# Two attention stages reordered: copies ahead of exponents, waits by head, negated scores, one multiplication on GpSimd

## The chip, the cores and the metric

One core of a Trainium2 chip runs the whole program. Its engines run side by side, each through its own queue of instructions: TensorE (PE), VectorE (DVE), ScalarE (ACT), GpSimd (POOL) and SyncE (SP), which issues most of the DMAs. They wait for each other on semaphores. The metric is the device time of one execution in microseconds (us). Before the change it is 3049.75 us, the median of 3 runs (3048.73 to 3050.3).

## The reference

The input is `x` of 512 tokens by 1024. A first block of two layers runs over it, each with a mixer, a cross attention and an MLP. The mixer of layer 0 has two self attentions, and these are the first stage that the change touches:

```python
# a: 4 heads, each with two maps (c = 0, 1) of 64 columns, values of 128 columns
p = softmax(where(causal, q_c @ k_c.T * scale, -inf))
out_a = (p[:, :, 0] - lam * p[:, :, 1]) @ va          # then an rmsnorm of each row
# b: 8 heads of 64 columns, keys chosen by an index (top_k)
p = softmax(where(chosen & causal, q @ k.T * scale, -inf)); out_b = p @ vb
```

A second block follows: modulation from `c`, an mLSTM mixer beside an attention with 8 heads of 64 columns over all 512 keys with a bias by distance (the second stage that the change touches), an output product, and 16 experts that choose 64 tokens each:

```python
xin = h[idx]; hid = silu(xin @ w_gate) * (xin @ w_up)
y = (hid @ w_down) * gates; x = x + gate2 * zeros.at[idx].add(y)
```

All is float32. The weights of the experts are 16 x 3 matrices of 1024 x 2048, some 403 MB, which are read once.

## The kernel before

The program is a row of blocks. In a block each engine has its own list of instructions, and at its end all engines meet. Weights come through a ring of four slots of 2 MB (`Program.prefetch`), and the order of the work on each engine is written out by hand.

**Attention.** `attend_steps` does a list of steps. A step is one tile of 128 queries for two things at a time (e = 0, 1): in "apart" steps the two maps of one head, whose outputs are kept apart and joined later, else two heads. Step s does in turn:

- PE `scores(s)`: two products into PSUM banks 0 and 1, or 2 and 3, by the parity of s. It waits until `peak(s - 2)` has read these banks.
- DVE `peak(s)` (L661): `tensor_tensor_reduce` adds the bias (causal mask or distance), scales, writes the scores to SBUF (`probs`) and takes the row maximum, once for each e. A small instruction (L665) then multiplies the two maxima by -1, after a wait for the one in front (`vlink`).
- ACT `exponent(s)` (L745): exp(score - maximum) for each e, with the row sums.
- DVE `mix(s)`, only for steps that aren't apart (L672, L675): the reciprocal of the sums, then both heads' probabilities multiplied by it.
- PE `turn(s)` (L606): the probabilities transposed 128 x 128 at a time into banks 4 (e = 0) and 5 (e = 1). It waits for the probabilities of s, and for both copies of step s - 1, which read the same two banks.
- ACT and DVE `copy_turned(s)` (L754, L682): bank 4 to SBUF by ACT; bank 5 by ACT in even steps and by DVE in odd ones.
- PE `values(v)` (L620 apart, L626 else): the product with the values, once for each apart step and once for two steps else. DVE `finish(v)` (L689, L693 to L697) moves the result out.

The steps are staggered by `lag`: in its round s, PE does scores(s), turn(s - lag) and then values of a group that ended at s - lag - 1. DVE does peak(s), mix(s - 1), its copy of s - lag, finish. ACT does exponent(s), then its copies of s - lag, and in the first stage a row of squares (`square`).

There are two calls. `e_att` (in `even_mixer`, lag 3) has 32 steps: 16 apart (4 heads by 4 tiles of queries) and 16 not apart (4 pairs of heads by 4 tiles); tile i of queries has (i + 1) x 128 keys, so widths go 128, 256, 384, 512 and start again. While the second 16 run, DVE also does the rmsnorm of the first half's rows (`row_scale`, `scale_rows`). `s_att` (in `second_block`, lag 2) has 16 steps, none apart, all of width 512.

**Experts.** `experts` follows `s_att`. It streams 8 pairs of experts x 24 chunks of 2 MB through 8 slots. The output product of the mixer and the router run first, in the same block. Of the last pair, `scatter_half(0)` (L2945) adds the first half of the columns of the result back to the token rows: PE spreads it (four tiles of tokens), DVE adds (L3029, `add_half`). It stands between the two last groups of products of the last column half. DVE's order is: first half gated, its four adds, second half gated (L3060), its four adds.

## Time and profile before

| What | Value |
|---|---|
| Median of 3 runs | 3049.75 us |
| Profiled execution, own time | 3044.21 us |
| Its span, first to last instruction | 3042.4 us |
| PE busy | 2820.1 us (93%) |
| DVE, ACT, POOL busy | 779.3, 431.1, 56.6 us |
| DMA | 570.71 MB, 188 GB/s over the span |
| Mean granted TensorE clock | 0.981 of full speed |
| `e_att`, first scores to the next stage's first product | 264.80 to 369.01 us |
| `s_att`, the same | 1954.24 to 2025.07 us |

The page has a line of tenths for each engine in 40 slices of the span. DMA stands at 9 from slice 29 on (427 to 429 GB/s), the stage of the experts, and at 0 to 3 in most others. The busy share of PE hides stretches in which it runs on with short gaps, as in the two attention stages; these are seen in the views by stretch and by time.

### The profile page before, as it was taken

How to read it: one execution, taken by the hardware profiler on the slowest of the kernel's cores; microseconds unless marked ns; L12 is line 12 of the kernel's file. 1: busy time of each engine (PE TensorE's matmuls, PEld its weight loads, DVE VectorE, ACT ScalarE, POOL GpSimd, SP SyncE). 2: the span in 40 equal slices, each digit the busy share in tenths (PEclk: the TensorE clock that was granted, in tenths of full speed). 3: DMA queues.
4: the chain of work that ended last, by engine and by line, in shares of the span. 5: the costliest groups of instructions: out<-in, count | busy, mean ns of one | idle time of the engine just before them, and what ended most of it. 6: DMA issues, size and time to landing. Idle time of an engine off the chain costs nothing. (4 is left out here: it accounts for less than half of the span.)

```text
span 3042.4 us, 24643 instructions
## 1 busy us (share of the span) xinstructions
PE 2820.1 (93%) x9741; PEld 1277.8 (42%) x9741; DVE 779.3 (26%) x1998; ACT 431.1 (14%) x950; POOL 56.6 (2%) x149
## 2 busy tenths in 40 slices
PE   8998898999999998999999899787999889889888
PEld 4545544444444444444544444444333323233232
DVE  2398623011001314340000244644111111111111
ACT  2124412000001002211000122231000000000000
POOL 0000000000000000110000010000000000000000
PEclk9999999999999999999999999898999999999999
DMA  7230012122212201682121111222999999999998
GB/s 279 69 111 14 1 42 83 61 77 83 83 62 80 83 28 56 210 287 83 56 83 56 55 57 56 76 84 103 427 428 428 428 428 429 428 428 428 428 428 374
DMA packets 107472, 570.71 MB, mean 188 GB/s; under 512 B 11578, under 2 KB 12364, under 8 KB 82940
## 3 DMA queue, kind: packets, MB, share of 16 engines
q1 hardware_dynamic: 99248, 538.64, 44.0%
q0 software_dynamic: 6768, 29.43, 2.8%
q10 hardware_dynamic: 1372, 1.51, 0.2%
q8 instruction: 54, 0.88, 0.1%
q14 instruction: 30, 0.25, 0.0%
HBM read 567.43 MB, written 6.32 MB: 189 GB/s over the span
## 5 line engine op out<-in xcount | busy, mean ns | idle before, releaser
L205 PE MATMUL banks<-hT,ring 128*128 128x512 f32 x1024 | 441.5, 594 | 5.1 <-PEq L298 5.1
L205 PEld LDWEIGHTS banks<-hT,ring 128*128 128x128 f32 x1024 | 195.0, 191 | 250.4 <-issue 250.4
L2902 PE MATMUL banks<-ring,second_arena 128*64 128x512 f32 x1024 | 232.0, 597 | 29.7 <-DMA ring<-in_w_up 16.0
L324 PE MATMUL banks<-ring,m_u 128*128 128x512 f32 x512 | 220.3, 592 | 1.6 <-PEq L178 1.6
L1984 PE MATMUL banks<-ring,second_arena 128*128 128x512 f32 x512 | 220.6, 593 | 0.0
L2902 PE MATMUL banks<-second_arena 128*64 128x512 f32 x768 | 174.5, 598 | 17.5 <-DMA second_arena<-in_w_gate 15.0
L324 PEld LDWEIGHTS banks<-ring,m_u 128*128 128x128 f32 x512 | 97.0, 190 | 123.4 <-issue 123.4
L1984 PEld LDWEIGHTS banks<-ring,second_arena 128*128 128x128 f32 x512 | 97.5, 191 | 121.7 <-issue 121.7
L2902 PEld LDWEIGHTS banks<-ring,second_arena 128*64 128x64 f32 x1024 | 70.0, 136 | 184.0 <-issue 133.6
L2902 PE MATMUL banks<-ring,mod 128*64 128x512 f32 x512 | 114.7, 596 | 12.7 <-DMA ring<-in_w_down 12.7
L3022 DVE TENSOR_TENSOR x_rows<-banks,x_rows 128x512 f32<-128x512 f32 x64 | 44.3, 692 | 282.4 <-PE banks L2938 282.4
L1749 PE MATMUL banks<-hT,ring 128*128 128x512 f32 x256 | 110.4, 592 | 2.5 <-PEq L298 2.5
L1523 PE MATMUL banks<-ring,hT 128*128 128x512 f32 x256 | 111.1, 594 | 0.9 <-PEq L887 0.9
L2902 PEld LDWEIGHTS banks<-second_arena 128*64 128x64 f32 x768 | 51.2, 136 | 133.3 <-issue 89.5
L2902 PE MATMUL banks<-second_arena,mod 128*64 128x512 f32 x384 | 84.6, 595 | 2.9 <-DMA second_arena<-in_w_down 2.9
L3051 DVE TENSOR_TENSOR mod<-banks,mod 128x512 f32<-128x512 f32 x32 | 22.1, 691 | 244.5 <-PE banks L2902 244.5
L360 ACT ACTIVATE x_square<-x_rows 128x1024 f32<-128x1024 f32 x20 | 21.1, 1057 | 401.5 <-DVE x_rows L348 217.1
L1899 DVE SCALAR_TENSOR_TENSOR mod<-second_arena,mod 128x1536 f32<-128x1536 f32 x32 | 58.2, 1819 | 75.0 <-DMA second_arena<-in_w_ada 75.0
L1749 PEld LDWEIGHTS banks<-hT,ring 128*128 128x128 f32 x256 | 48.5, 190 | 63.0 <-issue 63.0
L1523 PEld LDWEIGHTS banks<-ring,hT 128*128 128x128 f32 x256 | 48.6, 191 | 62.0 <-issue 61.2
L2902 PE MATMUL banks<-hT,second_arena 128*64 128x512 f32 x256 | 58.3, 597 | 14.9 <-DMA hT<-in_w_up 14.9
L2938 PE MATMUL banks<-second_arena 128*128 128x512 f32 x128 | 72.0, 645 | 0.0
(563 smaller groups left out, 2897.0 us busy)
## 6 DMA issues: line engine op xcount, KB each, us to landing
ring<-in_w_up SPq DMA_DIRECT2D x48, 2048.0 KB, 30.5
ring<-in_w_down SPq DMA_DIRECT2D x48, 2048.0 KB, 33.7
ring<-in_w_gate SPq DMA_DIRECT2D x32, 2048.0 KB, 34.0
second_arena<-in_w_gate SPq DMA_DIRECT2D x32, 2048.0 KB, 30.7
second_arena<-in_w_down SPq DMA_DIRECT2D x24, 2048.0 KB, 35.4
second_arena<-in_w_up SPq DMA_DIRECT2D x16, 2048.0 KB, 32.4
hT<-in_w_up SPq DMA_DIRECT2D x16, 2048.0 KB, 33.8
second_arena<-in_w_ada POOLq DMA_DIRECT2D x32, 768.0 KB, 4.7
```

The lines of the kernel that those rows point to most:

```text
L205: mm = nc.tensor.matmul(o, w[:, k, a:z], src[:, ka, 0:ntok], start=(ka == 0), stop=(ka == kc * kgroups - 1))
L324: mm = nc.tensor.matmul(g.psum[:, b * NT + m, :], act[:, ka, m * P:m * P + P], w[:, k, :], start=(ka == 0), stop=(ka == kc * kgroups - 1))
L360: g.alink(nc.scalar.activation(square[:], g.x[:, t, :], ACT.Square, accum_out=g.row_stats[:, 0, t:t + 1]))
L1523: mm = nc.tensor.matmul(bank, a[:, k, m * P:m * P + P], w[:, k, :], start=(k == 0), stop=(k == kc - 1))
L1749: mm = nc.tensor.matmul(o, w[:, k, m * P:m * P + P], g.hT[:, k, :], start=(k == 0), stop=(k == KD - 1))
L1899: nc.vector.scalar_tensor_tensor(o, w[:, n % 2, :], cs[:, k:k + 1], o, ALU.mult, ALU.add).then_inc(added.up(), 1)
L1984: mm = nc.tensor.matmul(g.psum[:, b * NT + m, :], u[:, ka, m * P:m * P + P], w[:, k, :], start=(ka == 0), stop=(ka == KD * kgroups - 1))
L2902: mm = nc.tensor.matmul(g.psum[64 * e:64 * e + 64, bank, :], lhs(q * half + k)[:, 64 * e:64 * e + 64], w[:, e, k, :], start=first, stop=last)
L2938: nc.tensor.matmul(g.psum[:, 6 + u % 2, :], sg[:, tt * P:tt * P + P], y[:, c * BANK:c * BANK + BANK], start=True, stop=True).then_inc(s_ba ...
L3022: nc.vector.tensor_tensor(xs, g.psum[:, 6 + u % 2, :], xs, ALU.add).then_inc(s_add.up(), 1)
L3051: nc.vector.tensor_tensor(hid[:, b % 2, :], g.psum[:, (b % 2) * 2 + 1, :], act_g[:, b % 2, :], ALU.mult).then_inc(s_hid.up(), 1)
```

## The change

In `attend_steps`: ACT does its copies of step s - lag before the exponents of step s. DVE's copies are left only in apart odd steps; in all others ACT makes both. PE waits for the copy of bank 4 before it turns e = 0, and for that of bank 5 only before e = 1. `peak` scales by -scale and takes a minimum, so that its result is the negated maximum; L665 and its wait go, and the exponent is taken with scale = -1. In steps that aren't apart DVE multiplies only head 0 by the reciprocal; a new list of GpSimd does head 1, and PE waits for both. The argument `warm`, which no caller sets, goes. In `experts`, two of the four tiles of `scatter_half(0)` move behind the last group of products.

```diff
--- before.py
+++ after.py
@@ -534,7 +534,7 @@
                     at += a
 
 
-def attend_steps(g, name, steps, probs, keyed, scale, lag, warm=0, rows=None):
+def attend_steps(g, name, steps, probs, keyed, scale, lag, rows=None):
 
     nc = g.nc
     S, B = len(steps), 4
@@ -548,18 +548,17 @@
     mixed_before = [sum(not st["apart"] for st in steps[:s + 1]) for s in range(S)]
     s_scores, s_peak, s_probs, s_mixed, s_turned, s_out, s_read, s_copied_a, s_copied_v = (g.counter(n) for n in (
         "scores", "peak", "probs", "mixed", "turned", "out", "out_read", "moved_a", "moved_v"))
+    s_inverse, s_mixed_pool = g.counter("inverse"), g.counter("rooted")
     s_joined, s_squared, s_scaled, s_rows_turned = (g.counter(n) for n in ("joined", "squared", "scaled", "x_turned"))
 
-    def copied_by_act(s):
-        return s + 1 + s // 2 + 1
-
-    def copied_by_dve(s):
-        return (s + 1) // 2
-
-    def wait_copied(eng, s):
-        eng.wait_ge(*s_copied_a.at(copied_by_act(s)))
-        if s:
-            eng.wait_ge(*s_copied_v.at(copied_by_dve(s)))
+    by_dve = [st["apart"] and s % 2 for s, st in enumerate(steps)]
+
+    def wait_copied(eng, s, e):
+        n = sum(by_dve[:s + 1])
+        if e and by_dve[s]:
+            eng.wait_ge(*s_copied_v.at(n))
+        else:
+            eng.wait_ge(*s_copied_a.at(2 * s + e + 1 - sum(by_dve[:s])))
 
     def into(s, e):
         step = steps[s]
@@ -599,9 +598,10 @@
                         pe.wait_ge(*s_probs.at(s + 1))
                     else:
                         pe.wait_ge(*s_mixed.at(mixed_before[s]))
-                    if s:
-                        wait_copied(pe, s - 1)
+                        pe.wait_ge(*s_mixed_pool.at(mixed_before[s]))
                     for e in range(2):
+                        if s:
+                            wait_copied(pe, s - 1, e)
                         for j in range(step["nk"] // P):
                             mm = nc.tensor.transpose(g.psum[:, 4 + e, j * P:j * P + P], probs[:, s % B, e, j * P:j * P + P],
                                                      g.ident[:])
@@ -609,7 +609,8 @@
 
                 def values(v):
                     step = steps[ops[v][-1]]
-                    wait_copied(pe, ops[v][-1])
+                    for e in range(2):
+                        wait_copied(pe, ops[v][-1], e)
                     if v >= 2:
                         pe.wait_ge(*s_read.at(v - 1))
                     n = step["nk"] // P
@@ -630,9 +631,6 @@
                 for s in range(S + lag + 1):
                     if s < S:
                         scores(s)
-                    if s == 0:
-                        for _ in range(warm):
-                            nc.tensor.matmul(g.psum[:, 7, :], g.ident[:], g.causal[:, 0:BANK], start=True, stop=True)
                     if 0 <= s - lag < S:
                         turn(s - lag)
                     if s - lag - 1 in last_of:
@@ -646,6 +644,14 @@
                                                          g.ident[:])
                             mm.then_inc(s_rows_turned.up(), 1)
 
+            @block.gpsimd
+            def _(pool):
+                for s in range(S):
+                    if not steps[s]["apart"]:
+                        pool.wait_ge(*s_inverse.at(mixed_before[s]))
+                        p = probs[:, s % B, 1, 0:steps[s]["nk"]]
+                        nc.gpsimd.tensor_scalar(p, p, st[:, s % 8, 3, 1:2], None, ALU.mult).then_inc(s_mixed_pool.up(), 1)
+
             @block.vector
             def _(dve):
                 v_ = nc.vector
@@ -659,21 +665,19 @@
                         if "ready" in step:
                             dve.wait_ge(*step["ready"][e])
                         ins = v_.tensor_tensor_reduce(probs[:, s % B, e, 0:step["nk"]],
-                                                      g.psum[:, (s % 2) * 2 + e, 0:step["nk"]], step["bias"][e], scale,
-                                                      NEG * 10, ALU.add, ALU.max, st[:, s % 8, 0, e:e + 1])
-                    g.vlink(ins)
-                    v_.tensor_scalar(st[:, s % 8, 1, :], st[:, s % 8, 0, :], -1.0, None, ALU.mult).then_inc(s_peak.up(), 1)
+                                                      g.psum[:, (s % 2) * 2 + e, 0:step["nk"]], step["bias"][e], -scale,
+                                                      -NEG * 10, ALU.add, ALU.min, st[:, s % 8, 1, e:e + 1])
+                    ins.then_inc(s_peak.up(), 1)
 
                 def mix(s):
                     step = steps[s]
                     if step["apart"]:
                         return
                     dve.wait_ge(*s_probs.at(s + 1))
-                    g.vlink(v_.reciprocal(st[:, s % 8, 3, :], st[:, s % 8, 2, :]))
-                    for e in range(2):
-                        p = probs[:, s % B, e, 0:step["nk"]]
-                        ins = v_.tensor_scalar(p, p, st[:, s % 8, 3, e:e + 1], None, ALU.mult)
-                    ins.then_inc(s_mixed.up(), 1)
+                    v_.reciprocal(st[:, s % 8, 3, :], st[:, s % 8, 2, :]).then_inc(s_inverse.up(), 1)
+                    dve.wait_ge(*s_inverse.at(mixed_before[s]))
+                    p = probs[:, s % B, 0, 0:step["nk"]]
+                    v_.tensor_scalar(p, p, st[:, s % 8, 3, 0:1], None, ALU.mult).then_inc(s_mixed.up(), 1)
 
                 def copy_turned(s):
                     dve.wait_ge(*s_turned.at(2 * s + 2))
@@ -722,7 +726,7 @@
                         peak(s)
                     if 1 <= s <= S:
                         mix(s - 1)
-                    if 0 <= s - lag < S and (s - lag) % 2:
+                    if 0 <= s - lag < S and by_dve[s - lag]:
                         copy_turned(s - lag)
                     if s - lag - 2 in last_of:
                         finish(last_of[s - lag - 2])
@@ -742,7 +746,7 @@
                     act.wait_ge(*s_peak.at(s + 1))
                     for e in range(2):
                         p = probs[:, s % B, e, 0:step["nk"]]
-                        ins = nc.scalar.activation(p, p, ACT.Exp, bias=st[:, s % 8, 1, e:e + 1],
+                        ins = nc.scalar.activation(p, p, ACT.Exp, bias=st[:, s % 8, 1, e:e + 1], scale=-1.0,
                                                    accum_out=st[:, s % 8, 2, e:e + 1])
                     ins.then_inc(s_probs.up(), 1)
 
@@ -764,12 +768,12 @@
                 if rows:
                     act.wait_ge(*s_joined.at(1))
                 for s in range(S + lag):
+                    if s >= lag:
+                        copy_turned(s - lag, 0)
+                        if not by_dve[s - lag]:
+                            copy_turned(s - lag, 1)
                     if s < S:
                         exponent(s)
-                    if s >= lag:
-                        copy_turned(s - lag, 0)
-                        if not (s - lag) % 2:
-                            copy_turned(s - lag, 1)
                     if rows and 0 <= s - lag - 3 < apart:
                         square(s - lag - 3)
                 if rows:
@@ -2938,10 +2942,10 @@
                 nc.tensor.matmul(g.psum[:, 6 + u % 2, :], sg[:, tt * P:tt * P + P], y[:, c * BANK:c * BANK + BANK],
                                  start=True, stop=True).then_inc(s_back.up(), 1)
 
-            def scatter_half(c):
+            def scatter_half(c, tiles=range(NT)):
 
                 pe.wait_ge(s_y.sem, (pairs - 1) * 2 + (s_y.base + c + 1))
-                for tt in range(NT):
+                for tt in tiles:
                     nc.tensor.matmul(g.psum[:, last_banks[c][tt], :], sg[:, tt * P:tt * P + P],
                                      y[:, c * BANK:c * BANK + BANK], start=True, stop=True).then_inc(s_back.up(), 1)
 
@@ -2964,8 +2968,8 @@
                     for kg in range(2):
                         pair_of_groups(i, 4 * nf + 4 * b + 2 * kg, 6 + b, lambda k: hT[:, kg * KD + k, :],
                                        kg == 0, kg == 1, last and b == kg == 1)
-                        if last and b == 1 and kg == 0:
-                            scatter_half(0)
+                        if last and b == 1:
+                            scatter_half(0, (2 * kg, 2 * kg + 1))
                     if b == 0 and not last:
                         gather(i + 1)
 
```

## Rows read from the trace of the kernel before

**Rows 1.** Chain that ended last, in order of time: start us, us, what.

```profile
2272.85 32.10 DMA ring<-in_w_down
```

**Rows 2.** Stretches: us, then each engine busy (x instructions), PEclk, DMA share, GB/s.

```profile
2110.00:2125.00 15.00, 13.68 (x84) 11.01 (x86) 4.44 (x12) 0.00 (x0) 0.00 (x0) 0.79 0.00 1
2125.00:2272.00 147.00, 145.22 (x672) 52.52 (x670) 19.14 (x32) 9.62 (x14) 0.00 (x0) 1.00 1.00 424
```

**Rows 3.** Stretches of attention, same view; engines PE, PEld, DVE, ACT, POOL.

```profile
305.76:317.75 11.99, 10.29 (x78) 7.97 (x77) 9.72 (x44) 7.42 (x31) 0.00 (x0) 1.00 0.01 2
317.75:333.59 15.84, 13.01 (x83) 8.11 (x82) 12.89 (x58) 8.06 (x31) 0.00 (x0) 0.89 0.00 1
333.59:346.06 12.47, 8.21 (x47) 4.67 (x45) 11.23 (x42) 6.62 (x22) 0.00 (x0) 0.86 0.01 2
346.06:356.73 10.67, 8.35 (x62) 4.86 (x61) 9.42 (x39) 6.50 (x22) 0.00 (x0) 1.00 0.00 0
...
1978.87:1986.57 7.70, 6.09 (x43) 3.38 (x41) 5.69 (x18) 4.49 (x12) 0.00 (x0) 1.00 0.00 0
```

**Rows 4.** Instructions in order of time, first stage: start us, us, engine, line.

```profile
308.97 0.49 PE L592 MATMUL banks<-e_KTb,e_QTb 64*128 64x128 f32 x4
...
309.91 0.42 ACT L754 ACTIVATE e_keyed<-banks 128x128 f32<-128x128 f32 x2
...
310.42 0.63 PE L606 MATMUL banks<-ident,e_probs 128*128 128x128 f32 x4 [0.96 <-ACT e_probs L745]
```

**Rows 5.** Instructions in order of time, one pair of steps of the second stage.

```profile
1978.87 1.13 PE L592 MATMUL banks<-second_arena 64*128 64x512 f32 x4
...
1980.05 0.69 DVE L661 CUSTOM_DVE_ANT_0 second_arena<-banks,second_arena 128x512 f32<-128x512 f32 x1 [1.86 <-PE banks L592]
...
1981.27 0.08 DVE L661 DVE_READ_ACCUMULATOR2_ANT s_att_stats<- 128x1 f32 x1
1981.39 0.17 DVE L665 TENSOR_SCALAR s_att_stats<-s_att_stats 128x2 f32<-128x2 f32 x1
1981.47 0.16 DVE L672 RECIPROCAL s_att_stats<-s_att_stats 128x2 f32<-128x2 f32 x1
1981.60 0.72 ACT L745 ACTIVATE second_arena<-second_arena,s_att_stats 128x512 f32<-128x512 f32 x1 [1.88 <-DVE s_att_stats L665]
1981.66 0.88 DVE L675 TENSOR_SCALAR second_arena<-second_arena,s_att_stats 128x512 f32<-128x512 f32 x2
...
1983.02 0.58 ACT L754 ACTIVATE mod<-banks 128x512 f32<-128x512 f32 x1
...
1983.69 1.06 PE L606 MATMUL banks<-ident,second_arena 128*128 128x128 f32 x8 [1.61 <-ACT mod L754]
...
1984.69 1.95 PE L626 MATMUL banks<-mod,second_arena 128*64 128x256 f32 x16
...
1986.57 1.13 PE L592 MATMUL banks<-second_arena 64*128 64x512 f32 x4
```

**Rows 6.** GpSimd: in order of time beside DVE; one group by line; a DVE tile view.

```profile
1914.27 2.29 DVE L2309 TENSOR_TENSOR second_arena<-second_arena,s_head_stats 128x2048 f32<-128x2048 f32 x1
1914.42 2.29 POOL L2165 TENSOR_SCALAR_AFFINE_SELECT second_arena<-second_arena 128x128 f32<-128x128 f32 x1 [9.33 <-DVE second_arena L2349]
...
L909 POOL TENSOR_SCALAR_AFFINE_SELECT causal<-causal 128x512 f32<-128x512 f32 x1 | 0.6, 612 | 0.1
...
L675 DVE TENSOR_SCALAR e_probs<-e_probs,e_att_stats x32: 279/383/486, 313.5 to 359.7; 128x128 f32<-128x128 f32 x8, 128x256 f32<-128x256 f32 x8, 128x384 f32<-128x384 f32 x8, 128x512 f32<-128x512 f32 x8
```

**Rows 7.** Instructions in order of time, the end of the kernel.

```profile
3024.04 3.70 PE L2945 MATMUL banks<-second_arena 128*128 128x512 f32 x8
...
3027.67 3.65 PE L2902 MATMUL banks<-second_arena,mod 128*64 128x512 f32 x16
...
3034.81 0.69 DVE L3060 TENSOR_TENSOR second_arena<-banks,mod 128x512 f32<-128x512 f32 x1 [6.34 <-PE banks L2902]
...
3035.56 3.70 PE L2945 MATMUL banks<-second_arena 128*128 128x512 f32 x8 [0.80 <-DVE second_arena L3060]
```

## The prediction

> **What bounds the kernel now.** I read the chain of waits first. From 2272.85 us on it is the stream of expert weights that sets the pace: PE is released by a landing each time [rows 1]. So the question is whether time won earlier reaches the end. The view by stretches answers it: DMA stands still from 2110 to 2125 us (share 0.00), and from 2125 on it runs full (1.00) without a break [rows 2]. The stream therefore starts when PE, in the expert stage, frees its first slot, and not before. Whatever ends earlier ahead of it moves the stream as one piece. The same holds between the two attention stages, which are PE's own product stages with weights loaded ahead. A microsecond won in attention is a microsecond at the end.
>
> Then the attention stages, by stretches cut at the same point of each round of four steps. In the first half of `e_att` a round is 11.99 us with PE busy 10.29; in the second half three rounds are 15.84, 12.47 and 10.67 us, with PE busy 13.01, 8.21 and 8.35; in `s_att` a pair of steps is 7.70 us with PE busy 6.09 [rows 3]. No engine is full; the time is in waits that go round. Last, the instructions in order of time show which. In `e_att` scores of width 128 start at 308.97 and the next turn only at 310.42, after a wait of 0.96. Its missing input is a copy of the step before, which ACT starts at 309.91, behind two long exponents, though PE had finished that turn by 308.97 [rows 4]. In `s_att` it is the same: ACT copies at 1983.02, behind the exponents that began at 1981.60, and PE turns at 1983.69 after 1.61 us idle [rows 5].
>
> **The change, part by part.** Each term is a saving (minus) or a cost (plus) in us.
>
> *First stage, apart steps (4 rounds).* No GpSimd work here. With ACT's copies ahead of the exponents, a copy starts when its turn is done. The wait by head lets PE turn e = 0 while bank 5 is still being copied, and the path from scores to exponent loses L665. What is late next: PE itself, which has 10.29 busy us in a round, against DVE 9.72 and ACT 7.42 [rows 3]. DVE loses four L665 of 0.17 [rows 5]. So a round goes to about 10.29: 4 x (11.99 - 10.29) = -6.8. If the exponents pushed back by the copies were late for PE three steps on, some of it would stay; lag 3 leaves room.
>
> *First stage, steps not apart (4 rounds, three whole ones in the rows).* DVE now loses, per round, four L665 (0.17), four multiplications (0.28 to 0.49, median 0.38 [rows 6]) and two copies: some 2.2 us besides the copies. DVE's 12.89, 11.23 and 9.42 busy us [rows 3] become at most 10.7, 9.0 and 7.2. ACT takes the two copies, and the pair at 309.91 and the single one at 1983.02 put a copy between 0.2 and 0.6 us [rows 4, 5]; ACT's 6.62 becomes 7.8 at most, still under PE. The bound of each round is then the larger of PE and DVE: 13.01, 9.0, 8.35. That saves 2.8 + 3.5 + 2.3 = 8.6. The rmsnorm of the rows is a serial run on DVE that PE waits for, and it stays, so I take -7.0 of it. The fourth round, filling and draining: the last copies and the last mix are shorter for PE, -1.
>
> *Second stage (16 steps).* The loop after the change, per pair, by [rows 5]: scores to the first DVE operation 1.18 (1978.87 to 1980.05); two reductions to the start of the reciprocal, now without L665, 1.30 (1980.05 to 1981.27, and 0.08); reciprocal to multiplication 0.19; the slower of the two multiplications 1.0 (next paragraph) and 0.05 to PE; turn 1.00 (1983.69 to 1984.69); values 1.88 (to 1986.57), after which come the next scores of this kind. Together 6.60. PE's own work is 6.09, ACT's 4.49 plus one copy of 0.58, DVE's 5.69 less two L665, two multiplications and a copy. So the loop sets it: 7.70 - 6.60 = 1.10 a pair, over seven and a half pairs: -8.2.
>
> *The GpSimd multiplication.* The trace has no such operation. The nearest row is a one-input select of 128x512 with 0.612 [rows 6]. One row shows what happens beside DVE: a select of 128x128 took 2.29 us while DVE ran an operation of 2.29 on two SBUF tensors, and ended 0.15 after it [rows 6]. DVE's multiplication goes from 0.28 at 128 columns to 0.49 at 512, 0.5 ns a column, two columns a cycle of the one-column rate of 0.69 us at 512 that the reduction has [rows 5, 6]. If that form also shuts GpSimd out, head 1 starts when head 0 is done: 0.44 + 0.56 = 1.0 after the reciprocal, no better than the 0.88 that DVE takes for both [rows 5]. If not, it is 0.61 to 0.65. Ends: 0.6 (the loop falls to 6.2, -11.2 in the second stage) and 2.3 (the blocked row; the loop is 7.9, +1.5). I take 1.0. In the first stage lag 3 gives the multiplication a whole further step, so it costs nothing there below about 2.5 us.
>
> The Trainium skill bears on this (SBUF — State Buffer, Who interferes with whom): a DVE instruction in a 2-port mode and a GpSimd instruction exclude each other for their whole length, and `tensor_scalar` can be in such a mode. The blocked row agrees for two SBUF inputs. By the rule the GpSimd part wins nothing here, and without it the second stage would stand at -11.2 rather than -8.2.
>
> *The end.* Before, the four products of `scatter_half(0)` run from 3024.04 to 3027.67 and PE idles while L3060 runs at 3034.81 [rows 7]. Two of them (0.9 each) go behind the last products. PE then ends these 1.8 earlier and spreads tiles 2 and 3 until about 3034.8. But DVE adds all four tiles before it gates the second half: L3060 waits for the add of tile 3, which starts at about 3034.8 and takes 0.6 to 0.7. The last spread starts at 3036.2 instead of 3035.56: +0.65. If the last landing holds PE up, it loses up to the 1.8 as well: +2.5. I take +0.7.
>
> *Sum.* -6.8 - 7.0 - 1.0 - 8.2 + 0.7 = -22.3. The profiled execution took 3044.2 (span 3042.4), so it would be 3021.9. It lies 5.5 below the median of 3049.75, and I carry the difference over: 3027.5.
>
> The granted clock is at the lower level for part of these stages (0.89 and 0.86 in two rounds [rows 3]) after PE idled. Shorter idles may bring it back, and a new one may cost it; two or three us either way, not in the sum.
>
> **The rivals.**
>
> *A, GpSimd free of DVE and the clock steadier.* The loop is then 6.2 a pair and near PE's 6.09: 3 more, and 2 to 4 from the clock. For it: the reductions, which read one tensor from PSUM, should not stand in GpSimd's way. Against: the blocked row. Time 3021.
>
> *B, half of it.* The waits between engines that my loops leave out, ACT's later exponents and the new double wait before each turn (PE's whole queue stands behind it: turn, values, and the scores two steps on) take half of the gain, so -12: 3038. For it: DVE and ACT would be above 80% busy in some rounds, which leaves little slack. Against: the loops add up to the rounds before.
>
> *C, slower.* One mechanism: GpSimd's multiplication. In `s_att` each us of it beyond 1.0 costs 7.5 in all; in `e_att` it starts to count at about 2.5 and then costs some 8 per us. At 2.0 the second stage has lost its gain; at about 3.2 it costs 16 there and 6 in the first, and the whole change stands at zero. At 3.6 it is 3055. For it: only the blocked select of 2.29. Against: 0.612 for the same width.
>
> *D, nothing reaches the end.* The expert stream decides and the start of the stream doesn't move, or the change doesn't shorten the rounds. 3050.5. Against: DMA share 0.00 before 2125 [rows 2].
>
> **How the numbers follow.** Forecast (-17 to -27): 0.58, A 0.16, B 0.16, C 0.05, D 0.05. A measurement of this kernel can tell about 0.2%, 6.1 us, from no change. Faster by more: the forecast, A, and B but for its weak end, 0.90; within: D and the rest of B, 0.06; slower: 0.04. The range runs from A's better end, 3018, to B's weaker one, 3041; some 0.06 lie below and 0.12 above.
>
> **What would show it.** In the profile after: rounds of `e_att` of 10.2 to 10.6 us in the first half and 8.5 to 10.5 in the second; pairs of `s_att` of 6.6 (6.2 would show rival A); ACT's copies (now ahead of L745) starting within 0.1 us of their turn; GpSimd's multiplication ending about 1.0 after the reciprocal, behind DVE's; no gap of 1.4 us after the scores of width 128. L3060 starts behind an add of L3029. The stages between should keep their length, and the expert stage too, within 1 us. A GpSimd row above 2 us, a DMA that no longer stands still before the stream, or rounds still at 12 and 7.7 would prove the prediction wrong.

## The result, and the profile after

The changed kernel took 3024.74 us (median of 4 runs, 3020.18 to 3028.71) against 3050.03 us of the kernel before on the same chip (3048.73 to 3051.51): a ratio of 0.9916 [0.9899, 0.9934], 25.3 us less. It ran twice more later, at 3026.08 us (ratio 0.9929 [0.9912, 0.9946]) and 3023.19 us (0.9917 [0.9903, 0.993]). The forecast was 3027.5, 22.3 us less.

The profiled execution took 3026.5 us, with a span of 3024.8. I cut both spans at the same four instructions: first scores of `e_att`, first product of the stage behind it, first scores of `s_att`, first product behind it.

| Stretch, us | before | after | change | forecast |
|---|---|---|---|---|
| ahead of `e_att` | 264.80 | 265.21 | +0.41 | 0 |
| `e_att` | 104.21 | 82.33 | -21.88 | -14.8 |
| between the two, untouched | 1585.23 | 1592.69 | +7.46 | 0 |
| `s_att` | 70.83 | 67.28 | -3.55 | -8.2 |
| from there to the end | 1017.33 | 1017.29 | -0.04 | +0.7 |
| span | 3042.4 | 3024.8 | -17.6 | -22.3 |

So the sum came out near the forecast, but its terms did not: the first stage gave half as much again, the second less than half. The two errors (7.1 too small, 4.7 too large) have opposite signs and partly cancel in the sum, which is luck. And the stretch that nothing in the change touches is 7.5 us longer in this pair of profiles.

The view by stretches of the kernel after, for the second and fourth round of apart steps, the three rounds behind them, a pair of steps of `s_att`, each whole stage and the stretch between (us, then busy time of PE, PEld, DVE, ACT, POOL, then the granted clock, DMA share and GB/s):

```profile
276.77:286.98 10.21, 10.21 (x77) 7.97 (x76) 8.37 (x35) 7.82 (x32) 0.00 (x0) 1.00 0.01 2
297.19:307.40 10.21, 10.21 (x77) 7.97 (x76) 8.74 (x38) 7.82 (x32) 1.71 (x2) 1.00 0.01 2
307.40:315.73 8.33, 8.33 (x61) 5.64 (x60) 7.66 (x32) 6.04 (x27) 4.08 (x4) 1.00 0.00 1
315.73:326.47 10.74, 8.54 (x62) 4.95 (x61) 10.15 (x42) 7.94 (x28) 5.99 (x4) 1.00 0.01 2
326.47:334.96 8.49, 8.25 (x62) 4.87 (x61) 7.08 (x28) 7.16 (x25) 4.98 (x4) 1.00 0.00 1
1972.80:1980.29 7.49, 6.09 (x43) 3.38 (x41) 3.98 (x13) 4.97 (x13) 3.71 (x2) 1.00 0.00 0
265.21:347.54 82.33, 75.59 (x561) 53.36 (x561) 65.00 (x262) 61.41 (x218) 21.18 (x16) 1.00 0.01 1
347.54:1940.23 1592.69, 1530.30 (x4000) 722.65 (x4001) 339.76 (x789) 211.54 (x441) 50.07 (x107) 0.98 0.24 84
1940.23:2007.51 67.28, 53.03 (x321) 29.66 (x321) 32.44 (x104) 40.14 (x96) 29.84 (x17) 0.93 0.00 1
```

Against [rows 3]: a round of apart steps is 10.21 us and PE is busy in all of it (11.99 and 10.29 before). The pair of `s_att` went only from 7.70 to 7.49, and POOL is now busy 3.71 of it, two multiplications.

The three rounds behind it, 8.33, 10.74 and 8.49 us, can't be set against the 15.84, 12.47 and 10.67 of [rows 3]. Those three aren't cut at the same point of their rounds: they hold 83, 47 and 62 products of PE, those of the kernel after 61, 62 and 62. The same view of the kernel before, first its four last rounds, each from one set of scores of width 512 to the next (the last to the end of the stage) as in the view above, then its first round, the two halves of `e_att`, and `s_att`:

```profile
317.75:329.32 11.57, 9.88 (x61) 6.54 (x60) 9.07 (x39) 6.28 (x26) 0.00 (x0) 0.85 0.00 1
329.32:343.46 14.14, 9.87 (x62) 5.73 (x61) 12.52 (x52) 6.62 (x22) 0.00 (x0) 0.88 0.01 2
343.46:354.72 11.26, 8.35 (x61) 4.86 (x60) 9.94 (x42) 6.72 (x23) 0.00 (x0) 1.00 0.00 0
354.72:369.01 14.29, 9.79 (x81) 7.01 (x81) 8.14 (x22) 6.42 (x17) 0.00 (x0) 1.00 0.00 1
264.80:281.76 16.96, 13.72 (x72) 8.88 (x72) 10.26 (x48) 9.56 (x34) 0.00 (x0) 0.76 0.01 1
264.80:317.75 52.95, 44.61 (x301) 32.81 (x301) 38.13 (x167) 32.62 (x124) 0.00 (x0) 0.92 0.01 1
317.75:369.01 51.26, 37.89 (x261) 24.14 (x261) 39.67 (x152) 26.03 (x87) 0.00 (x0) 0.93 0.00 1
1954.24:2025.07 70.83, 55.51 (x320) 30.52 (x321) 45.91 (x144) 36.14 (x88) 0.09 (x1) 0.89 0.00 1
```

So these rounds went from 11.57, 14.14, 11.26 and 14.29 to 8.33, 10.74, 8.49 and 12.58 (334.96 to 347.54). Of the first three, only the middle one still has PE waiting for more than 0.3 us. It holds DVE's rmsnorm, and DVE is busy for 10.15 of its 10.74. In order of time, PE waits in it first for DVE and then for GpSimd:

```profile
320.82 0.70 PE L591 MATMUL banks<-e_KTb,e_QTb 64*128 64x256 f32 x4 [0.69 <-DVE e_att_stats L667]
323.02 0.85 PE L606 MATMUL banks<-ident,e_probs 128*128 128x128 f32 x6 [1.50 <-POOL e_probs L653]
```

Compare the granted clock: 0.92 and 0.93 over the two halves of `e_att` before, 1.00 over the whole of it after. PE's busy time for the same instructions fell with it, from 82.50 (44.61 + 37.89) to 75.59. A part of that is no effect of the change. The first scores of the stage, the same 16 products, kept PE busy for 4.95 us before and 2.75 after, though the stage had hardly waited by then. In before's profile the clock stood at 0.50 (1.2 GHz) in the stage's first 3 us, in after's at 1.00 (2.4 GHz). These are the rows of before, then of after:

```profile
264.80 4.95 PE L592 MATMUL banks<-hT 64*128 64x128 f32 x16 [0.94 <-PEq L1503]
...
265.21 0.93 PE L591 MATMUL banks<-hT 64*128 64x128 f32 x8 [1.29 <-PEq L1507]
266.40 1.82 PE L591 MATMUL banks<-hT 64*128 64x384 f32 x8 [0.26 <-DVE e_att_stats L667]
```

The first turn follows 4.87 us after the stage's start before and 2.94 after, so some 1.9 of the 21.88 us belong to that one execution. Experiment 1 below, which has the change's order of copies, begins at 0.50 as well.

Instructions in order of time, `s_att` after (start us, us, engine, line; in brackets the idle time ahead and its releaser). These answer to [rows 5]:

```profile
1972.80 1.13 PE L591 MATMUL banks<-second_arena 64*128 64x512 f32 x4
...
1975.21 0.16 DVE L677 RECIPROCAL s_att_stats<-s_att_stats 128x2 f32<-128x2 f32 x1
1975.40 0.48 DVE L680 TENSOR_SCALAR second_arena<-second_arena,s_att_stats 128x512 f32<-128x512 f32 x1
1975.46 1.85 POOL L653 TENSOR_SCALAR second_arena<-second_arena,s_att_stats 128x512 f32<-128x512 f32 x1 [3.48 <-DVE s_att_stats L677]
...
1977.41 1.06 PE L606 MATMUL banks<-ident,second_arena 128*128 128x128 f32 x8 [1.40 <-issue]
...
1978.08 1.08 ACT L758 ACTIVATE mod<-banks 128x512 f32<-128x512 f32 x2 [1.04 <-PE banks L606]
1978.41 1.95 PE L627 MATMUL banks<-mod,second_arena 128*64 128x256 f32 x16
```

DVE's half is ready at 1975.88, GpSimd's at 1977.31, and PE turns at 1977.41 after 1.40 us idle. The row names "issue", but what ends just in front of it is GpSimd's half; a later profile of the same kernel (experiment 4) names it at the same place of an earlier pair:

```profile
1953.66 1.06 PE L606 MATMUL banks<-ident,second_arena 128*128 128x128 f32 x8 [1.40 <-POOL second_arena L653]
```

In the rows of the kernel after, ACT's copies are no longer late: they start at 1978.08, while the turn (1977.41 to 1978.47) still runs.

The end of the kernel after, against [rows 7]:

```profile
3005.56 1.98 PE L2949 MATMUL banks<-second_arena 128*128 128x512 f32 x4
3007.48 3.65 PE L2906 MATMUL banks<-second_arena,mod 128*64 128x512 f32 x16
...
3016.52 0.69 DVE L3033 TENSOR_TENSOR x_rows<-banks,x_rows 128x512 f32<-128x512 f32 x1 [0.17 <-PE banks L2949]
3017.12 0.68 DVE L3064 TENSOR_TENSOR second_arena<-banks,mod 128x512 f32<-128x512 f32 x1
...
3017.86 3.70 PE L2949 MATMUL banks<-second_arena 128*128 128x512 f32 x8 [1.38 <-DVE second_arena L3064]
...
3021.60 0.69 DVE L3033 TENSOR_TENSOR x_rows<-banks,x_rows 128x512 f32<-128x512 f32 x1 [0.17 <-PE banks L2949]
```

The gate L3064 starts right behind an add, as foreseen. From the first spread to the end of the last add it is 3022.29 - 3005.56 = 16.73 us; before, it was 15.94 (from 3024.04 to the last add's end at 3039.98).

### The profile page after: what moved, and what is told of

The parts are those of the page before. It is cut to its first block and busy times, and to the rows that moved or that the text cites. A ratio compares the mean times of both kernels' runs of the same rounds, so it can differ in the third digit from the quotient of the medians.

```text
span 3024.8 us, 24597 instructions
## 1 busy us (share of the span) xinstructions
PE 2816.1 (93%) x9741; PEld 1275.1 (42%) x9741; DVE 753.2 (25%) x1902; ACT 437.9 (14%) x966; POOL 107.3 (4%) x181
## 5 line engine op out<-in xcount | busy, mean ns | idle before, releaser
L2906 PE MATMUL banks<-second_arena 128*64 128x512 f32 x768 | 174.5, 598 | 17.6 <-DMA second_arena<-in_w_gate 15.1
L2906 PE MATMUL banks<-hT,second_arena 128*64 128x512 f32 x256 | 58.3, 597 | 14.8 <-DMA hT<-in_w_up 14.8
```

Source lines behind the costliest of these rows:

```text
L2906: mm = nc.tensor.matmul(g.psum[64 * e:64 * e + 64, bank, :], lhs(q * half + k)[:, 64 * e:64 * e + 64], w[:, e, k, :], start=first, stop=last)
```

## The experiments

The theory after the first result: ACT's copies behind the exponents held PE up in both stages, and putting them first is most of the gain; in `s_att` GpSimd's multiplication of 1.86 us has taken the place of that wait. The rivals: the gain comes from the parts that shorten DVE's work (negation, multiplication), or the length of the multiplication does not matter. Except where it is said, each kernel is the changed one with one edit.

**1. Both multiplications on DVE.**

```diff
-                    p = probs[:, s % B, 0, 0:step["nk"]]
-                    v_.tensor_scalar(p, p, st[:, s % 8, 3, 0:1], None, ALU.mult).then_inc(s_mixed.up(), 1)
+                    for e in range(2):
+                        p = probs[:, s % B, e, 0:step["nk"]]
+                        ins = v_.tensor_scalar(p, p, st[:, s % 8, 3, e:e + 1], None, ALU.mult)
+                    ins.then_inc(s_mixed.up(), 1)
```

GpSimd's list and PE's wait for it go.

> The changed kernel, but VectorE multiplies both heads again and GpSimd does nothing in attention. Stage lengths are from the first scores to the next block's first product: first stage 104.2 us before and 82.3 after, second stage 70.8 and 67.3. Theory 1 (GpSimd's 1.86 us a multiplication sets the loop of the second stage): its pair of steps falls from 7.49 us to 5.58 + 0.88 = 6.46, at least PE's 6.09; the second stage falls by some 7 to 59 to 61 us, the first stage grows by 0 to 3 because VectorE is fuller beside the row work. Total 3 to 8 us faster than the changed kernel. Theory 2 (taking work off VectorE is where the gain comes from): the second stage grows to 69 or more and the first by over 5; total 5 or more slower than the changed kernel.

Measured: 3020.15 us (4 runs, 3018.66 to 3020.42), ratio 0.9904 [0.9887, 0.992]; `e_att` 85.45, `s_att` 57.03 us. In order of time, one pair of `s_att`:

```profile
1968.84 1.13 PE L591 MATMUL banks<-second_arena 64*128 64x512 f32 x4
...
1971.44 0.88 DVE L672 TENSOR_SCALAR second_arena<-second_arena,s_att_stats 128x512 f32<-128x512 f32 x2
...
1972.37 1.09 PE L605 MATMUL banks<-ident,second_arena 128*128 128x128 f32 x8 [0.33 <-DVE second_arena L672]
...
1975.27 1.13 PE L591 MATMUL banks<-second_arena 64*128 64x512 f32 x4
```

The pair is 6.43 us (1975.27 - 1968.84), PE's idle ahead of the turn 0.33 instead of 1.40. The two multiplications together are done 0.88 after they start, GpSimd's one after 1.85. So GpSimd's multiplication costs `s_att` 10 us (67.28 - 57.03; 8.4 and 11.0 against the two later profiles of the changed kernel), while the stage without it would have gained 13.8. Theory 1 is borne out, and by more than it named: the second stage fell below its 59 to 61 us. The 85.45 of `e_att` holds the low clock at its start, as before's does; experiment 12, the same kernel, took 83.58.

**2. Exponents first, as before the change.**

```diff
+                    if s < S:
+                        exponent(s)
                     if s >= lag:
                         copy_turned(s - lag, 0)
                         if not by_dve[s - lag]:
                             copy_turned(s - lag, 1)
-                    if s < S:
-                        exponent(s)
```

> The changed kernel, but ScalarE does the exponents of step s ahead of its copies of the step before by lag, as before the change. Theory 1 (the order on ScalarE is the main gain of the first stage): the first stage goes back from 82.3 to 90 to 96 us and the waits of 1.0 and 0.7 us of PE in each round of four steps return; the second stage stays within 1.5 us of 67.3, as GpSimd holds it anyway. Total 8 to 12 slower than the changed kernel. Theory 2 (the gain is from the negation that went, the wait by head and the multiplication that moved): first stage below 86.

Measured: 3043.22 us (8 runs, 3037.89 to 3044.5), ratio 0.998 [0.997, 0.9991]; `e_att` 94.30, `s_att` 69.28. The old wait is back in both stages:

```profile
306.34 0.19 ACT L749 ACTIVATION_READ_ACCUMULATOR e_probs<-e_probs,e_att_stats 128x1 f32 x1
306.43 0.42 ACT L758 ACTIVATE e_keyed<-banks 128x128 f32<-128x128 f32 x2
...
306.83 0.63 PE L606 MATMUL banks<-ident,e_probs 128*128 128x128 f32 x4 [0.64 <-ACT e_keyed L758]
...
1977.50 1.06 PE L606 MATMUL banks<-ident,second_arena 128*128 128x128 f32 x8 [1.45 <-ACT mod L758]
```

ACT copies at 306.43, behind the exponent of 512 columns, and PE turns once the copy is done. The order of ACT's list alone is worth 17 us of the 25 (3043.22 against 3026.08 of the changed kernel on the same chip), more than the 8 to 12 expected. In `s_att` it is worth little while GpSimd is in the loop: the turn waits 1.45 for the copy or 1.40 for GpSimd.

**3. Both multiplications on GpSimd.**

```diff
-                        pe.wait_ge(*s_mixed.at(mixed_before[s]))
-                        pe.wait_ge(*s_mixed_pool.at(mixed_before[s]))
+                        pe.wait_ge(*s_mixed_pool.at(2 * mixed_before[s]))
```

GpSimd's list goes over e = 0 and 1, and DVE's multiplication goes.

> The changed kernel, but GpSimd multiplies both heads and VectorE none. It prices the multiplication without a VectorE one beside it. If VectorE's multiplication holds GpSimd off for its length, the first of each two GpSimd rows of 512 columns takes about 1.86 - 0.43 = 1.4 us where no other VectorE work lies beside it. If 1.86 is GpSimd's own time, both rows stay at 1.8 to 1.86. The second stage then pays two of them in its loop: pair 5.58 + 3.7 = 9.3 us, second stage 81 to 84 us; with 1.4 each 8.4 and 75 to 77 us.

Measured (one run): 3051.51 us; `e_att` 86.38, `s_att` 87.61. Groups of GpSimd's multiplication by form (busy us, mean ns | idle before), both on GpSimd:

```profile
L653 POOL TENSOR_SCALAR second_arena<-second_arena,s_att_stats 128x512 f32<-128x512 f32 x32 | 49.5, 1564 | 56.9 <-DVE s_att_stats L678 56.9
L653 POOL TENSOR_SCALAR e_probs<-e_probs,e_att_stats 128x384 f32<-128x384 f32 x8 | 10.2, 1290 | 5.9 <-DVE e_att_stats L678 5.9
L653 POOL TENSOR_SCALAR e_probs<-e_probs,e_att_stats 128x128 f32<-128x128 f32 x8 | 4.8, 606 | 280.3 <-DVE e_att_stats L678 280.3
```

And the same groups of the kernel after, where DVE multiplies beside it:

```profile
L653 POOL TENSOR_SCALAR second_arena<-second_arena,s_att_stats 128x512 f32<-128x512 f32 x16 | 29.7, 1854 | 56.7 <-DVE s_att_stats L677 56.7
...
L653 POOL TENSOR_SCALAR e_probs<-e_probs,e_att_stats 128x384 f32<-128x384 f32 x4 | 6.4, 1600 | 9.0 <-DVE e_att_stats L677 9.0
L653 POOL TENSOR_SCALAR e_probs<-e_probs,e_att_stats 128x128 f32<-128x128 f32 x4 | 3.2, 798 | 280.7 <-DVE e_att_stats L677 280.7
```

Without DVE's multiplication beside it GpSimd takes 1.56 us for 512 columns, with it 1.85. So 1.56 is its own time, and 0.29 is what DVE's multiplication of 0.48 adds. Neither expected case is what `s_att` shows: 87.61 lies above both (75 to 77 and 81 to 84). It is 20 us longer than with one multiplication on GpSimd. PE's busy time for the same products grew by 10 of them (53.03 to 63.22), with the granted clock at 0.81 over the stage (0.93 with one), which the expectation left out. The first stage, with its lag of three steps, grows by 3 to 4.

**4. The changed kernel once more.** No edit.

> The changed kernel once more, unaltered, on the chip of the three others, so that they can be compared with it. Stage lengths 82.3 and 67.3 us within 2, total within 4 of 3024.7; differences between executions should lie in stretches at the lower clock level elsewhere.

Measured: 3026.08 us (4 runs, 3025.81 to 3030.22), ratio 0.9929 [0.9912, 0.9946]; `e_att` 83.39, between 1592.60, `s_att` 65.47. A third time (run 11 below): 83.47, 1587.00 and 68.02. The stretch between, of the same kernel in its second and its third profile:

```profile
348.14:1940.74 1592.60, 1530.17 (x4001) 724.22 (x4001) 339.73 (x789) 211.55 (x441) 50.52 (x107) 0.98 0.24 84
```

```profile
349.32:1936.32 1587.00, 1524.64 (x4000) 720.26 (x4001) 339.46 (x789) 211.44 (x441) 50.48 (x107) 0.98 0.24 84
```

The same instructions differ by 5.6 us, and PE's busy time by 5.5. Over all profiles this stretch took 1585 to 1587 (before, 9, 10, 11) or 1592 to 1595 (the rest), and the unaltered changed kernel stands in both groups. So the +7.46 of the first table needs no effect of the change; whether a kernel makes one of the two lengths more likely, these profiles do not show.

**5. The kernel before, with nothing but the copies put first.** The edit is that of experiment 2, the other way round, in the kernel before.

> The kernel before, with one edit: ScalarE's copies of a step ahead of the exponents. Theory 1: this alone brings the first stage from 104.2 to 91 to 97 us, and the second from 70.8 to 66 to 69. Theory 2 (the parts only work together, or the order matters little): first stage above 100.

Measured (one run): 3032.74 us beside 3049.69 for before; `e_att` 93.61, `s_att` 63.29. In order of time, this kernel:

```profile
314.66 1.12 PE L606 MATMUL banks<-ident,e_probs 128*128 128x128 f32 x6 [1.58 <-DVE e_keyed L682]
...
1984.63 1.06 PE L606 MATMUL banks<-ident,second_arena 128*128 128x128 f32 x8 [1.21 <-DVE mod L682]
```

One reordering gives 17 us. What remains is DVE: in the steps that aren't apart PE waits for DVE's copy (L682), behind its two multiplications. The other parts together give some 6 more (3032.74 against 3026.42 of experiment 7, on the same chip). That is a sum of two signs: they take 10 to 11 us off `e_att`, and they make `s_att` 2 to 5 us longer (63.29 here, 65.47 to 68.02 with the whole change), since GpSimd's multiplication is one of them. In `e_att` the two are nearly additive: 104.21 - 93.61 = 10.6 and 104.21 - 94.30 = 9.9, together 20.5, and 20.7 to 21.9 were measured with both. Each of these differences holds the 1.9 us of before's low clock at the start.

**6. The negation kept as an instruction.**

```diff
-                                                      g.psum[:, (s % 2) * 2 + e, 0:step["nk"]], step["bias"][e], -scale,
-                                                      -NEG * 10, ALU.add, ALU.min, st[:, s % 8, 1, e:e + 1])
-                    ins.then_inc(s_peak.up(), 1)
+                                                      g.psum[:, (s % 2) * 2 + e, 0:step["nk"]], step["bias"][e], scale,
+                                                      NEG * 10, ALU.add, ALU.max, st[:, s % 8, 0, e:e + 1])
+                    g.vlink(ins)
+                    v_.tensor_scalar(st[:, s % 8, 1, :], st[:, s % 8, 0, :], -1.0, None, ALU.mult).then_inc(s_peak.up(), 1)
```

> The changed kernel with the maximum and the small multiplication by -1 back, with its wait. Theory 1: the second stage's loop gets 0.1 to 0.2 us a pair longer, 67.3 to 68.3; the first stage 1 to 2 us longer. Rival: in the first stage PE is the bound and nothing changes (below 0.5), the negation being off the path there.

Measured (one run): 3035.22 us, `e_att` 84.54, `s_att` 70.45, the stretch between 1594.61. The pair of `s_att`:

```profile
1978.30:1985.98 7.68, 6.08 (x43) 3.37 (x41) 4.30 (x15) 4.98 (x13) 3.71 (x2) 1.00 0.00 0
```

It is 0.19 longer than 7.49, so the instruction and its wait cost 1.4 us over seven and a half pairs. `e_att` is 2.2 longer than the 82.33 of the changed kernel; the granted clock is 1.00 over the stage in both, so the clock isn't what parts them. The 70.45 of `s_att` is above the 67.3 to 68.3 expected. The rest of that difference lies in stretches at the lower clock (0.90 over the stage, 0.93 in the changed kernel). Of the 8.8 us that this run lies above experiment 7 on the same chip, 3.2 are in `s_att` and 2.8 in the stretch between, which the edit doesn't touch; one run cannot price the instruction closer.

**7. PE waits for both copies before it turns.**

```diff
-                    for e in range(2):
-                        if s:
+                    if s:
+                        for e in range(2):
                             wait_copied(pe, s - 1, e)
+                    for e in range(2):
```

> The changed kernel, but PE waits for both copies of the step before ahead of its first transposition, as before the change. Theory 1: with the copies early this wait is nearly always over: both stages within 0.7 us of 82.3 and 67.3. Rival (the wait by head carries a part of the gain): the first stage is 2 to 4 us longer.

Measured (one run): 3026.42 us; `e_att` 83.61, `s_att` 67.28. `e_att` is 0.6 beyond the bound of theory 1 (83.0), but the changed kernel itself took 83.39 and 83.47 in its other profiles. So one run shows no difference: with the copies first, the wait by head brings nothing by itself here.

**8. DVE's copies kept in all odd steps.**

```diff
-    by_dve = [st["apart"] and s % 2 for s, st in enumerate(steps)]
+    by_dve = [s % 2 for s, st in enumerate(steps)]
```

> The changed kernel, but in steps that aren't apart VectorE makes the bank 5 copy of odd steps again. Theory 1: the second stage stays within 1 us of 67.3, since GpSimd holds its loop; the second half of the first stage is 1 to 3 us longer, as VectorE has the row work there. Rival: ScalarE's extra copy costs as much as it saves, and both stages stay within 0.5.

Measured (one run): 3030.63 us; `e_att` 84.33, `s_att` 67.31. In `s_att` nothing changes, since GpSimd still sets its loop; `e_att` is 2.0 longer than the 82.33 of the changed kernel, both at a granted clock of 1.00, as theory 1 had it (one run). Of the 4.2 us that its time lies above experiment 7 on the same chip, 2.7 are in the stretch between (1594.44 against 1591.78).

**9 to 12. GpSimd where it is covered, and the end mended.** Experiment 9 gives the second stage back to DVE (`rows` is set in the first stage only):

```diff
-                        pe.wait_ge(*s_mixed_pool.at(mixed_before[s]))
+                        if rows:
+                            pe.wait_ge(*s_mixed_pool.at(mixed_before[s]))
...
-                    if not steps[s]["apart"]:
+                    if rows and not steps[s]["apart"]:
...
+                    for e in range(1 if rows else 2):
```

Experiment 10 is 9 and, in `experts`, the gate ahead of two adds:

```diff
                     if last:
-                        add_half(b)
+                        if b:
+                            add_half(0, (2, 3))
+                        add_half(b, (0, 1) if b == 0 else range(NT))
```

Run 11 is the changed kernel, 12 is experiment 1 again, all on one chip.

> The changed kernel with GpSimd's multiplication kept in the first stage only; in the second stage DVE multiplies both halves, as before the change. Theory (a multiplication on GpSimd pays where three steps of lag cover its 1.86 us and costs where the loop contains it): the first stage keeps its 82.3 to 83.4 us, the second falls from 65.5 to 67.3 to 57.0, its pair from 7.48 to 6.44 us, so the profiled span is 3015.5 (3014 to 3018) and the ratio to the kernel before about 0.989. Rival (the first stage gains nothing from GpSimd either, since PE is full in its first half): the first stage stands at 84 to 85.5, and the time equals that of both halves on DVE everywhere, 3020.

> As the run with GpSimd in the first stage only, and in the last pair DVE gates the second half of the products before it adds tiles 2 and 3 of the first. Theory (the last spread waits for the gate, and the gate stood behind two adds that wait for late spreads): the gate L3064 starts as soon as PE ends its last products, the idle of 1.38 us ahead of the last spread shrinks to about 0.7, and from the first spread to the end of the last add it is about 16.0 us instead of 16.7; time 0.7 below the run without it. Rival (the late adds only move behind and end the kernel later): 16.7 or more, no gain.

> The changed kernel as it is, as the partner of the other three on this chip. Expected: ratio to the kernel before 0.9916 to 0.993, first stage 82 to 84 us, second stage 65 to 68.

> Both halves multiplied by DVE in both stages, once more, to tell it from the run with GpSimd in the first stage only. Theory (GpSimd takes 0.28 to 0.49 us a step off DVE in the second half of the first stage, where DVE is the busiest engine beside PE): the first stage is 1.5 to 3 us longer than with GpSimd, the second the same 57.0, so 3020 against 3017. Rival: no difference that five rounds can tell.

| Kernel | us | ratio to before (3049.2) | `e_att` | between | `s_att` |
|---|---|---|---|---|---|
| 9 GpSimd in `e_att` only | 3012.33 | 0.9882 [0.9867, 0.9897] | 84.94 | 1585.22 | 57.03 |
| 10 the same, gate first | 3009.72 | 0.9871 [0.9855, 0.9886] | 83.39 | 1586.86 | 57.03 |
| 11 changed kernel | 3023.19 | 0.9917 [0.9903, 0.993] | 83.47 | 1587.00 | 68.02 |
| 12 both on DVE | 3018.94 | 0.9895 [0.988, 0.991] | 83.58 | 1594.95 | 57.01 |

The end of experiment 10, in order of time:

```profile
3000.38 5.42 PE L2952 MATMUL banks<-second_arena 128*128 128x512 f32 x12
...
3000.50 0.69 DVE L3067 TENSOR_TENSOR second_arena<-banks,mod 128x512 f32<-128x512 f32 x1 [6.34 <-PE banks L2909]
3001.54 0.69 DVE L3036 TENSOR_TENSOR x_rows<-banks,x_rows 128x512 f32<-128x512 f32 x1 [0.35 <-PE banks L2952]
...
3005.84 0.69 DVE L3036 TENSOR_TENSOR x_rows<-banks,x_rows 128x512 f32<-128x512 f32 x1 [0.17 <-PE banks L2952]
```

The gate now runs while PE spreads tiles 2 and 3, and PE does all its last spreads without a gap. From first spread (2991.45) to the last add's end it is 15.08 us, against 16.73 of the change and 15.94 of before: 1.65 gained, where 0.7 was expected.

The second stage came out as expected (57.03). The theory that GpSimd's half gains 1.5 to 3 us in the first stage isn't borne out: with GpSimd `e_att` took 82.33, 83.39, 83.47, 84.94 and 83.39 us, without it 85.45 and 83.58, and the two ranges overlap. The 84.94 of experiment 9 is above the 82.3 to 83.4 expected and holds more of the lower clock (0.96). The spans of 9 and 12 differ by 8.2 us in the profiles, and the stretch between, which neither touches, by 9.7. Two profiles have a granted clock of 1.00 over all of `e_att`: 82.33 with GpSimd, 83.58 without it. Of the 1.25 between them 1.0 lies in the third round of steps that aren't apart, where PE without GpSimd waits 1.21 for a copy of ACT. So GpSimd's half gains some 1 us in `e_att` in this one pair, and whether that is more than chance stays open. Experiment 10 beats both kernels: 39.5 us under before, 13.5 under the change, of which its profile places 11.0 in `s_att` and 1.65 at the end, beside that of run 11.

## Why the prediction was right, and where its terms were off

The time was 3024.7 against 3027.5 forecast. The mechanism is as written: PE waited for copies that stood behind exponents, and the time won reached the end. That the sum came within 3 us is partly luck, as a term of 14.8 was 7.1 too small and one of 8.2 was 4.7 too large. By its own steps:

- **What bounds the kernel.** Right. The first landing that PE waits for in the expert stream moved with the work ahead (2272.85 before, 2254.49 after): the stretch behind `s_att` kept its length (1017.33 and 1017.29), so the time won in attention reached the end.
- **First stage, apart steps (-6.8).** The round was forecast at 10.29 and is 10.21, bound by PE as stated. The term is mis-sized: the half fell from 52.95 to 42.19 (265.21 to 307.40), by 10.8. Three rounds gave 5.4. The first round alone gave another 5.4, from 16.96 at a granted clock of 0.76 to 11.56. I had priced it like the others at 1.7 and left the clock out of the sum. Of the 5.4, 1.9 came before the first turn, from a clock already low when the stage began; 1.7 is PE's first long wait for a copy (2.79 to 1.05), and the rest is PE at the lower clock behind that wait.
- **Steps not apart (-7.0) and the fourth round (-1.0).** Measured 11.1 (51.26 to 40.14). By rounds cut alike it is -3.2, -3.4, -2.8 and -1.7. The prediction's three rounds were not cut at the same point, though it says so, and its term for the first is a wrong reading: PE's 13.01 us of [rows 3] are 83 products, more than a round. By its own rule, cut alike, the first would have given 1.7 (11.57 - 9.88) and not 2.8, and even this floor was too high: the same 61 products took 9.88 us at a clock of 0.85 and 8.33 at 1.00. A busy time read at the lower clock is no floor. The second round was set by DVE and the waits behind it (10.15 busy), the third by PE (8.25 of 8.49). The fourth gave 1.7 where 1.0 was taken.
- **The clock, left out of the sum ("two or three us either way").** This is the failed part of the first stage's terms: they missed 7.1 us, and PE's busy time for the same products fell by 6.9 (82.50 to 75.59), about 2 of them from before's low start. PE's idle time fell by 15.0 (21.71 to 6.74), close to the 14.8 of the two terms together. The other two profiles of the changed kernel have 76.89 and 76.98.
- **Second stage (-8.2).** Measured -3.5, and -2.8 and -5.4 in the other two profiles of the same kernel (68.02 and 65.47). The loop was built rightly: its terms without the multiplication are 5.60, and with 1.86 they give 7.46 to the measured 7.49. Seven and a half pairs at 0.21 make 1.6 of the 3.5; the rest goes with PE's busy time, which fell by 2.5 for the same products (55.51 at a clock of 0.89, 53.03 at 0.93). The failed step is the price of GpSimd's multiplication, taken as 1.0 between 0.6 and 2.3. The split, 0.44 blocked by DVE and 0.56 of its own from a select of 0.612, had it the wrong way round: 1.56 of its own and 0.29 for DVE (experiment 3). This was rival C's mechanism, at a size at which it takes away more than half of the second stage's gain and not the whole change. With the multiplications on DVE the loop is 6.43, close to the 6.60 that the sum asked of GpSimd.
- **GpSimd's part in the first stage (nothing, lag 3 covers it).** Right but for one place. Rounds of 8.33 and 8.49 hold four multiplications of GpSimd with PE busy throughout or nearly so. In the round with the rmsnorm a turn waits 1.50 us and GpSimd is what releases it: one multiplication of 384 columns took 1.99 there. With both halves on DVE (experiment 12) the same turn waits 1.21 for ACT's copy, and the round is 10.84 instead of 10.74, so it cost nothing in sum.
- **The wait by head.** It was told together with the order of the copies. By itself it brings nothing (experiment 7); the order brings 17 us (experiments 2 and 5), the rest some 6, GpSimd's cost in `s_att` taken off.
- **The end (+0.7).** Right, +0.79 (15.94 to 16.73), by the mechanism described: the idle ahead of the last spread went from 0.80 to 1.38.
- **The offset of 5.5 us between profile and median.** I carried it over as if it belonged to the kernel. Most of it belonged to that one execution: the untouched stretch was 1585.23 in before's profile and 1592.69 in after's. All that lies outside that stretch gives 0.41 - 21.88 - 3.55 - 0.04 = -25.1, the medians -25.3. That they agree to 0.2 is chance, as the -21.88 holds the 1.9 named above. So the sum fell short by 3, and carrying the offset over did no harm.
- **The signs named.** Seen: rounds of 10.21 in the first half, ACT's copies that start once their turn is done, L3060's successor (L3064) behind an add, DMA almost still ahead of the stream (share 0.05 from 2092.43 to 2107.43). Just outside: rounds of 8.33 and 10.74 (8.5 to 10.5). Missed: the pair of `s_att` (6.6, measured 7.49), GpSimd's end about 1.0 behind the reciprocal (2.1, from 1975.21 to 1977.31), and the stretch between, which did not keep its length within 1 us.
- **Rival A** was half there: the clock steadied and gave more than the 2 to 4 us named, even without before's low start; GpSimd was not free. **Rivals B and D** did not come about. In B's favour only the round with the rmsnorm still waits.

## What to carry to other kernels

In a list written out by hand, put the short operation that frees a buffer for the bottleneck engine ahead of the long one that is needed only steps later; this one move gave 17 of the 25 us. Split work onto GpSimd only where the lag covers its whole length: the same instruction cost nothing that shows at three steps of lag and 10 us in a loop that contains it, so measure its length first, in its own form. Before two stretches are compared, count their instructions: 83 products are not the same round as 61. And before a busy time is used as a floor, read the granted clock of that stretch: at 0.76 to 0.93 part of it is clock. Much of that came back here when the waits went, and some of it was there before the stage began.

## What the runs showed of the hardware

- GpSimd's multiplication by one value per partition, float32, took 0.61, 0.96, 1.29 and 1.56 us for 128, 256, 384 and 512 columns, DVE's the 0.28 to 0.49 of [rows 6]. The Trainium skill (GPSIMD Engine Reference, 4.1 Engine selection) calls operations with one input "roughly line-rate" on GpSimd; measured, it is more than three times DVE's time at 512 columns.
- Beside a DVE multiplication of 0.48 us that starts 0.06 ahead, GpSimd's took 0.29 longer, not its whole remaining 0.42; DVE's own kept its 0.48 in `s_att`. The Trainium skill (SBUF — State Buffer, Who interferes with whom) says that the second of the two is blocked for the other's whole length; the direction agrees, the size is two thirds of it.
- A multiplication of 384 columns that also lay beside DVE's product of two SBUF tensors (0.68 us, L711) took 1.99 us on GpSimd, against 1.47 for the others of this width beside DVE's multiplication alone and 1.29 with neither (kernel after, experiment 3).
- Stretches at the lower of the two levels of TensorE's clock fall differently from one execution to the next of the same kernel: the same 4000 products took 1587.0 or 1592.6 us (experiments 11 and 4). The executions of the changed kernel ran from 3020.18 to 3030.22 us. By stage, cut at the same instructions, its three profiles lie within 1.2 us in `e_att` and 2.6 in `s_att`.
